# Key scores of the sample branch: four heads issued together from two buffers of turned keys, instead of one head between two transposes

## What is computed

```python
# selected branch: blocks that a top-k picked, keys read through a page table
s2 = jnp.einsum('bqhgd,bqhkrd->bqhgkr', qr_blk, k_b).astype(jnp.float32) * ATTN_SCALE
s2 = jnp.where(valid[:, :, :, None], s2, -jnp.inf)
p2 = jax.nn.softmax(s2.reshape(sh[:4] + (-1,)), axis=-1).reshape(sh)
o_sel = jnp.einsum('bqhgkr,bqhkrd->bqhgd', p2, v_b.astype(jnp.float32))
# window branch: the last 512 keys, no page table
o_win = band_attention(q_rot, kw_all, vw_all, w_off, C_WIN)
```

## Time and profile before

| | us |
|---|---|
| three runs: lowest, median, highest | 2061.18, 2064.89, 2072.67 |
| span of the profiled execution, first to last instruction | 2066.1 |
| stage of the sample keys in it, 1311.7 to 1623.2 | 311.5 |
| TensorE busy in that stage | 310.4 |
| DVE, ACT busy in that stage | 111.2, 96.2 |
| DMA in that stage | 129 GB/s |

### The profile page before, as it was taken

One profiled execution on the slowest core, in us unless ns is written; L12 is line 12 of the kernel. 1 busy time (PEld: TensorE's weight loads), 2 busy tenths in 40 slices (PEclk: granted clock), 3 DMA queues, 4 the chain that ended last, 5 costly groups with the idle time before them and its releaser, 6 DMA issues.

```text
span 2066.1 us, 43255 instructions
## 1 busy us (share of the span) xinstructions
PE 1915.6 (93%) x16603; PEld 1621.0 (78%) x16603; DVE 1063.6 (51%) x1777; ACT 833.9 (40%) x1761; POOL 1.4 (0%) x8
## 2 busy tenths in 40 slices
PE   4999999999999899998999997899999777879998
PEld 3899999888888799798999995444444467769998
DVE  3358777666443544346689665433333322235454
ACT  2344444554344333445755552333323322234454
POOL 0000000000000000000000000000000000000000
PEclk9999999999999799999999999999999899999999
DMA  5788878633877488576555552244444389885454
GB/s 192 232 269 263 263 257 265 206 113 123 267 263 247 146 280 272 203 233 202 157 151 162 162 155 75 92 139 132 136 130 136 116 286 295 286 280 188 170 179 139
DMA packets 306536, 406.05 MB, mean 197 GB/s; under 512 B 18472, under 2 KB 222823, under 8 KB 305088
## 3 DMA queue, kind: packets, MB, share of 16 engines
q1 hardware_dynamic: 306384, 403.94, 61.3%
HBM read 391.43 MB, written 12.45 MB: 195 GB/s over the span
## 4 chain that ended last, share of the span: by engine, by line
PE 77%; DVE 11%; SPq 4%; DMA 3%; issue 2%; ACT 2%; DVEq 0%; ACTq 0%
PE PJ L1541 44%; PE XB L1993 8%; PE XB L1567 4%; PE XB L2004 4%; DVE w_low L980 2%; SPq L490 2%; DVE scr L999 2%; SPq L496 1%; PE XB L1813 1%; PE PJ L1981 1%; PE XB L1656 1%; DMA cring<-in_cache_c_win_kv_dram 1%; PE PJ L1960 1%; PE XB L1585 1%; PE XB L2063 1%
## 5 line engine op out<-in xcount | busy, mean ns | idle before, releaser
L1541 PE MATMUL PJ<-xh,w_up 128*128 128x264 f32 x3072 | 920.2, 300 | 40.1 <-DVE w_low L980 21.5
L1541 PE MATMUL PJ<-xl,w_up 128*128 128x264 f32 x3072 | 881.0, 287 | 0.0
L1541 PE MATMUL PJ<-xh,w_low 128*128 128x264 f32 x3072 | 879.3, 286 | 0.0
L980 DVE TENSOR_TENSOR w_low<-wring,w_up 128x512 fp32r<-128x512 f32 x768 | 524.8, 691 | 606.0 <-ACT w_up L602 595.6
L602 ACT CAST w_up<-wring 128x512 fp32r<-128x512 f32 x768 | 473.3, 619 | 644.7 <-PE PJ L1541 536.9
L1541 PEld LDWEIGHTS PJ<-xh,w_up 128*128 128x128 f32 x3072 | 587.6, 191 | 79.8 <-issue 56.4
L1541 PEld LDWEIGHTS PJ<-xl,w_up 128*128 128x128 f32 x3072 | 587.7, 191 | 1.4
L1541 PEld LDWEIGHTS PJ<-xh,w_low 128*128 128x128 f32 x3072 | 585.6, 191 | 0.0
L1993 PE MATMUL XB<-wring,proj 128*32 128x512 f32 x320 | 167.1, 605 | 1.1 <-DVE proj L1419 0.9
L2004 PEld LDWEIGHTS XB<-const,cring 128*128 128x128 f32 x640 | 70.8, 141 | 86.1 <-ACT wring L926 41.9
L1412 DVE COPY wring<-XB 128x512 f32<-128x512 f32 x80 | 55.3, 691 | 159.6 <-PE XB L2004 159.6
(11 more groups left out here) (301 smaller groups left out, 1448.7 us busy)
## 6 DMA issues: line engine op xcount, KB each, us to landing
wring<-in_w_in_ab_dram SPq DMA_DIRECT2D x144, 512.0 KB, 4.6
cring<-in_cache_c_cmp_kv_dram SPq DMA_DIRECT2D x128, 512.0 KB, 3.9
cring<-in_cache_c_sel_kv_dram SPq DMA_DIRECT2D x256, 256.0 KB, 2.9
wring<-in_w_in_c_dram SPq DMA_DIRECT2D x112, 512.0 KB, 3.7
wring<-in_w_ple_gate_dram SPq DMA_DIRECT2D x64, 512.0 KB, 3.6
cring<-in_cache_a_kv_dram SPq DMA_DIRECT2D x48, 512.0 KB, 5.0
wring<-in_w_out_ab_dram SPq DMA_DIRECT2D x32, 512.0 KB, 5.2
cring<-in_cache_c_win_kv_dram SPq DMA_DIRECT2D x64, 256.0 KB, 4.1
```

What stands on the lines that cost most here:

```text
L980: nc.vector.tensor_tensor(w_low[:, e % NE], raw(e), w_up[:, e % NE].bitcast(F32), ALU.subtract).then_inc(sem("w_lo"), 1)
L1541: ins = nc.tensor.matmul(PJ[(2 * bl + c) % 4][:, 0:T], w[:, e % NE, k, tileT(c)], x[:, kx, :], start=(kx == 0 and w is w_up and x is xh), ...
```

## The change

`KTc` becomes a pair `KTs` of such buffers: the second lies in `kcmp[:, 0:4]`, whose compressed keys the kernel has used up by then. Sets take turns at the two. `key_scores` now goes by sets: it waits until all four copies of set n are made, issues the four matmuls of its heads one behind the other, and counts `kt_used` once for all four. It is called after the second step of the following set (h == 1), and no longer after every step. A copy waits for the scores of the set two before its own, instead of those of the step four before. `take_scores` moves from the first odd step of a chunk to the second. The transposes, the copies, the matmuls and the DMAs are the same in number and size, and SP's last wait asks for 40 instead of 160.

```diff
-        KTc = wring[:, 2:4].rearrange("p q k n -> p (q k n)").rearrange("p (h n) -> p h n", h=CH)
+        KTs = (wring[:, 2:4].rearrange("p q k n -> p (q k n)").rearrange("p (h n) -> p h n", h=CH),
+               kcmp[:, 0:4].rearrange("p b a d -> p (b a d)").rearrange("p (h n) -> p h n", h=CH))
...
-            sp.wait_ge(sem("kt_used"), K_STEPS)
+            sp.wait_ge(sem("kt_used"), 5 * B)
...
                     if k % 2 == 0:
                         act.wait_ge(sem("kt_T"), 8 + k + 1)
-                        if k >= CH:
-                            act.wait_ge(sem("kt_used"), k - CH + 1)
-                        nc.scalar.copy(KTc[:, k % CH, :], XB[1 + k % 3][:, :]).then_inc(sem("kt_even"), 1)
+                        if k >= 2 * CH:
+                            act.wait_ge(sem("kt_used"), k // CH - 1)
+                        nc.scalar.copy(KTs[k // CH % 2][:, k % CH, :], XB[1 + k % 3][:, :]).then_inc(sem("kt_even"), 1)
...
-                    if k % 32 == 1 and k > 32:
+                    if k % 32 == 3 and k > 32:
                         take_scores(k // 32 - 1)
                     if k % 2 == 1:
                         dve.wait_ge(sem("kt_T"), 8 + k + 1)
-                        if k >= CH:
-                            dve.wait_ge(sem("kt_used"), k - CH + 1)
-                        nc.vector.tensor_copy(KTc[:, k % CH, :], XB[1 + k % 3][:, :]).then_inc(sem("kt_odd"), 1)
+                        if k >= 2 * CH:
+                            dve.wait_ge(sem("kt_used"), k // CH - 1)
+                        nc.vector.tensor_copy(KTs[k // CH % 2][:, k % CH, :], XB[1 + k % 3][:, :]).then_inc(sem("kt_odd"), 1)
...
-                dve.wait_ge(sem("kt_used"), 32 * c + 32)
+                dve.wait_ge(sem("kt_used"), B * c + B)
...
-            def key_scores(k):
-                c, b, h = k // 32, k % 32 // CH, k % CH
-                if k % 32 == 0 and c >= 1:
+            def key_scores(n):
+
+                c, b = n // B, n % B
+                if b == 0 and c >= 1:
                     pe.wait_ge(sem("S_taken"), c)
-                pe.wait_ge(sem("kt_odd" if k % 2 else "kt_even"), k // 2 + 1)
-                nc.tensor.matmul(XB[0][32 * h:32 * h + 32, :], qzr[:, b, h, :], KTc[:, h, :],
-                                 start=(b == 0), stop=(b == B - 1), skip_group_check=True).then_inc(sem("kt_used"), 1)
+                pe.wait_ge(sem("kt_even"), 2 * n + 2)
+                pe.wait_ge(sem("kt_odd"), 2 * n + 2)
+                for h in range(CH):
+                    ins = nc.tensor.matmul(XB[0][32 * h:32 * h + 32, :], qzr[:, b, h, :], KTs[n % 2][:, h, :],
+                                           start=(b == 0), stop=(b == B - 1), skip_group_check=True)
+                ins.then_inc(sem("kt_used"), 1)
...
                     ins.then_inc(sem("kt_T"), 1)
-                    if k >= 1:
-                        key_scores(k - 1)
+                    if h == 1 and n >= 1:
+                        key_scores(n - 1)
...
-            key_scores(K_STEPS - 1)
+            key_scores(5 * B - 1)
```

## The result

| | before | changed kernel |
|---|---|---|
| median of the runs, us | 2065.71 | 2000.38 |
| lowest to highest | 2061.18 to 2072.67 | 1995.56 to 2003.44 |
| span of the profiled execution | 2066.1 | 1993.8 |
| stage of the sample keys: first transpose to the end of the last | 311.3 | 238.3 |

The ratio is 0.9684 (95%: 0.9658 to 0.971): 65 us less by the medians, between 60 and 71. The forecast was 75 us less, 1990 with a range from 1962 to 2018.

A forecast was written before the change was run, and what follows sets the result against it. TensorE's own work bound the sample keys stage; afterwards the DMA round trip would set the pace: 182 + 50 + 4 = 236 us instead of 311.5, so 2064.9 - 75 = 1990 us, range 1962 to 2018.

The forecast's parts named there:

- Four heads together: Scores of the sample keys on TensorE: a set's four heads take about 1.05 us, between 0.98 and 3.9.
- The row of the values stage: Neighbouring values matmuls, four heads in four partition groups: 32 passes of 128 columns in 1.08 us, a factor of 3.6.
- The second row: Compression of the first layer, read as the same overlap: 16 passes in 0.67 us instead of 1.96.
- The stage is TensorE's own until sets come late: Sample keys stage: only TensorE's work sets its 311.5 us; time taken off it shortens the kernel until something else is late.
- The round: Loading a page set, from its place's release through SP's issues and DMA landing to use: 7.4 us.
- The time in which TensorE works through the new set: TensorE in the sample keys stage: steps 1.1 + 1.1, scores 1.05, prompt pieces 1.25, in all 4.5 us.
- a term of its own: TensorE's clock in the sample keys stage: two or three falls at 1.7 us, 4 us more.
- Sum: Sample keys stage: 30 sets x 6.05 and ten x 5.0 us, 232, with clock falls 236; 75 us less.
- Costs that were put at nothing: Sample keys stage: later copies and `take_scores` cost nothing; without cover they would cost 10 and 6 us.
- The first (TensorE as pace): Sample keys stage: sets come quicker and TensorE sets the pace, 40 x 4.9 = 196 us, or 1949; chance 10%.
- The second: Scores on TensorE: heads half overlapped, 2015 us, chance 7%; not overlapped, 2063 and no gain, chance 3%.
- The third: TensorE's clock in the stage: half clock throughout, 2105 us, chance 4%; falls in one set of three, 2017, chance 8%.

The follow-up runs named there:

- one-group kernel: Changed kernel with the four heads of a set all writing the first 32 partitions of the score bank: 2048.2 us in one run.
- early lookup: SP reads a set's four page addresses before waiting for its place: on the changed kernel 1968.61 us, on the kernel before 2065.02 us in one run.
- three places: Changed kernel with a third place for a set of keys, so SP issues set n when the transposes of set n - 3 end: 1939.3 us.
- double lookup: Changed kernel with every page address looked up twice on SP, the first lookup unused: 2063.56 us in one run.
- one buffer: Changed kernel with one buffer of turned keys, so a set's copies wait until the scores of the set before are done: 2018.02 us.

## Why the prediction was right, and where its terms were off

**Four heads together: right.** Taken 1.05 us, measured 1.00 between starts. The row of the values stage was the right neighbour, and the one-group kernel with line 1907 shows that its reason (partition groups) was too: 3.62 us when it is taken away, inside the bound from above of 3.9. The second row that the prediction read as saying the same, 0.67 instead of 1.96, is a factor of 2.9 and not 3.6; taken at that it would have given 1.35 us.

**The stage is TensorE's own until sets come late: right.** Before, the early lookup is worth nothing; after, waits for sets are 40 us, as the prediction said (some 40).

**The round: right.** Taken 7.4 us; the thirty rounds of page sets in the trace of the changed kernel run from 7.1 to 11 with a median of 7.5, where the long ones are places that TensorE came to late rather than sets that came late.

**The time in which TensorE works through a set: right sum, wrong parts.** Taken 4.5, measured 4.7 as mean. At full clock it is 4.4 (three places, early lookup), so I had 0.1 too much work; and the clock adds 0.3. I had counted the clock in a term of its own, two or three falls and 4 us. The stage had six falls and 24 us at half clock. With 0.3 us on thirty sets the clock cost between 5 and 9 us by an estimate, half of it or all, as a longer set delays one of the two places or both. TensorE's pieces of work, added up from start to start, take 4.95 us a set here and 4.53 with three places, 17 us for the stage; how much of that lay on the path was not measured. So this term was mis-sized, by a factor of about two on the estimate, and the error in the own work hid some of it: that the stage came out within 3 us is luck in part. The double lookup shows the term when it grows: 28 us of work at the lower clock. The clock of the whole execution is 0.96, where 0.97 was forecast.

**Sum.** Predicted 6.05 and 5.0 us a set and 236 for the stage; measured 6.23 and 5.14, and 238. (For the window sets a round of 5 us was taken; they land 5.5 us after their place is free.) The stage lost 73 of the 75 us. By spans the whole lost 72.3. The medians lost 65, because the profiled execution of before was a slower one of its set (runs lie some 2 us above their span, so about 2068, an estimate, against a median of 2065.7) and that of after the quickest of its four (1995.6 against 2000.4). I had measured the sum against a single execution and moved it by 1.2 us to the median; that step was good for the stage and 7 us off for what the medians show. Why the changed kernel's runs lie wider (1989 to 2004 in eight runs) is open.

**Costs that were put at nothing: covered, nearly.** Waits for DVE's copies are 15 us of the weight load's time in 17 pieces of 0.8 or so; the matmuls themselves show no wait for them. With three places, where the waits for sets are gone and with them the cover, TensorE is still busy for 182 of 186 us, so the copies cost 4 us there at most.

**Rivals.** The first (TensorE as pace) is what the third place brings about: predicted 196 for that case, measured 186. By the starts in that trace it is the transposes that were put too high, 2.2 us a set against 1.94, and the scores a little, 1.05 against 0.97; the pieces of prompt units are 1.62 a set there as before the change, against 1.65 taken. The second was wrong as a whole: four heads take 1.00 us where one takes 0.98. The third showed its mechanism and not its size: by the Trainium skill (page "TensorE: Matmul & The Clock Gate", Part 4, PE-mode transpose) transposes should not bring the full clock; this case's trace disagrees: the clock rose from 0.51 to 0.99 behind 15 transposes with nothing between them. With three places the transposes of keys are 88 of 182 busy us, and the clock is 1.00, though there other matmuls stand between them. It fell behind waits, as the one of 2.67 us at 1411.40.

## What to carry to other kernels

In this kernel matmuls with 32 output partitions ran beside each other when they wrote different groups of 32 partitions and stood next to each other in the queue; four transposes between each two of them cost the whole of that, 2.9 us of 3.9 a set. When such a change takes two fifths off a stage's work (here 7.8 us a set to 4.6), compute the round of every buffer that feeds it (release, lookups, issues, landing) before and after: it can go from hidden to being the pace, as it did here, and the next gain, here nearly as large as the first (61 us against 65), then lies in one more place in the ring and not in the engine.

## What the runs showed of the hardware beyond what was expected

Waiting cost the clock as well, and not only waiting for sets: in the same work the granted clock of the stage was 1.00 where TensorE idled for 4 us (three places), 0.99 with 25 (early lookup), 0.95 with 40 (changed kernel), 0.91 with 56 (one buffer, of which 39 were waits for sets) and 0.85 with 70 (lookup twice). Of the others, those at 0.99 with under 5 us of idle time have their low piece at the very start, where it began before the stage. An address lookup on SP is dear, some 0.7 us for each of four, so that a set of one MB takes 3.85 us to issue with lookups between the issues, and 1.9 with page sets whose addresses were read early; window sets, which need none, take 1.77.
